# First mixer of a four-layer model: the head norm woven into the head loop, one root for six heads, the output product opened beside the last two heads

## What is computed

```python
def hgrn2_mixer(x, w_in, lb, head_gain, w_out):
    q, f_pre, i, g = jnp.split(x @ w_in, 4, axis=-1)
    ...                       # eight heads of width 128, chunks of 64 tokens, give o
    o = o * lax.rsqrt(jnp.mean(o * o, axis=-1, keepdims=True) + EPS)
    o = o * head_gain.astype(jnp.float32).reshape(A_HEADS, A_DV)
    o = o.reshape(Bsz, T, D_MODEL).astype(x.dtype) * jax.nn.silu(g)
    return o @ w_out
```

## Time and profile before

| | us |
|---|---|
| median of three runs | 1563.09 (1561.83 to 1564.55) |
| the profiled execution's own time | 1562.21 |
| its span in the trace | 1560.4 |
| TensorE busy | 1451.6 (93%) |
| VectorE busy | 1054.4 (68%) |
| ScalarE busy | 774.2 (50%) |

### The profile page before, as it was taken

One profiled execution on the slowest core, in us unless ns is written; L12 is line 12 of the kernel. 1 busy time (PEld: TensorE's weight loads), 2 busy tenths in 40 slices (PEclk: granted clock), 3 DMA queues, 4 the chain that ended last, 5 costly groups with the idle time before them and its releaser, 6 DMA issues. The chain is left out here.

```text
span 1560.4 us, 29022 instructions
## 1 busy us (share of the span) xinstructions
PE 1451.6 (93%) x11297; PEld 1392.3 (89%) x11297; DVE 1054.4 (68%) x1752; ACT 774.2 (50%) x1251; POOL 288.3 (18%) x390
## 2 busy tenths in 40 slices
PE   7998889999779997999988899989999988999997
PEld 7997889999678877999977799989999986899997
DVE  7764778886775536888777755367787666587643
ACT  6646545454454544555436555664433555544341
POOL 1001011210064420112001144002432100132110
PEclk9999999999898998999989999999999999999998
DMA  8533435569342213555962211136765733375451
GB/s 323 182 108 136 162 140 218 204 234 334 125 162 82 72 58 115 218 217 203 356 233 84 105 57 66 69 121 233 276 247 207 249 106 136 108 289 210 143 177 45
DMA packets 41860, 265.73 MB, mean 170 GB/s; under 512 B 4640, under 2 KB 5920, under 8 KB 16416
## 3 DMA queue, kind: packets, MB, share of 16 engines
q1 hardware_dynamic: 41760, 264.38, 46.8%
HBM read 263.31 MB, written 1.05 MB: 169 GB/s over the span
## 5 line engine op out<-in xcount | busy, mean ns | idle before, releaser
L224 DVE TENSOR_TENSOR w_lo<-raw,w_hi 128x2048 fp32r<-128x2048 f32 (+2 forms) x206 | 424.1, 2063 | 183.5 <-ACT w_hi L220 180.2
L220 ACT ACTIVATE w_hi<-raw 128x2048 fp32r<-128x2048 f32 (+2 forms) x223 | 384.1, 1727 | 82.0 <-PE bank L1081 43.0
L412 PE MATMUL bank<-x_hi_up,w_hi 128*128 128x272 f32 (+1 forms) x704 | 203.4, 289 | 8.3 <-DVE x_lo_up L717 8.1
L414 PE MATMUL bank<-x_hi_up,w_lo 128*128 128x272 f32 (+1 forms) x704 | 201.7, 287 | 0.0
L413 PE MATMUL bank<-x_lo_up,w_hi 128*128 128x272 f32 (+1 forms) x704 | 201.2, 286 | 0.0
L412 PE MATMUL bank<-z_hi,w_hi 128*128 128x258 f32 x704 | 200.3, 285 | 0.0
L413 PE MATMUL bank<-z_lo,w_hi 128*128 128x258 f32 x704 | 198.7, 282 | 0.0
L414 PE MATMUL bank<-z_hi,w_lo 128*128 128x258 f32 x704 | 198.0, 281 | 0.0
L412 PEld LDWEIGHTS bank<-x_hi_up,w_hi 128*128 128x128 f32 x704 | 133.3, 189 | 10.4 <-issue 8.8
L413 PEld LDWEIGHTS bank<-x_lo_up,w_hi 128*128 128x128 f32 x704 | 133.7, 190 | 0.0
L413 PEld LDWEIGHTS bank<-z_lo,w_hi 128*128 128x128 f32 x704 | 133.3, 189 | 0.1
(11 more groups left out here) (476 smaller groups left out, 3889.2 us busy)
## 6 DMA issues: line engine op xcount, KB each, us to landing
raw<-w_up SPq DMA_DIRECT2D x44, 1024.0 KB, 4.8
raw<-w_gu SPq DMA_DIRECT2D x44, 1024.0 KB, 4.8
work<-w_ada SPq DMA_DIRECT2D x27, 1024.0 KB, 5.0
raw<-w_down SPq DMA_DIRECT2D x32, 704.0 KB, 5.0
raw<-w_dn SPq DMA_DIRECT2D x32, 704.0 KB, 4.1
mod_w_down<-w_ada SPq DMA_DIRECT2D x16, 1024.0 KB, 6.1
raw<-w_a_in SPq DMA_DIRECT2D x15, 1024.0 KB, 5.0
raw<-w_gdn_qkv SPq DMA_DIRECT2D x12, 1024.0 KB, 4.9
```

The lines of the kernel that those rows point to most:

```text
L220: act.activation(w_hi[:, s, 0:blocks * P], raw[:, s, 0:blocks * P], ACT.Copy).then_inc(hi_split.sem, 1)
L224: dve.tensor_tensor(w_lo[:, s, 0:blocks * P], raw[:, s, 0:blocks * P], w_hi[:, s, 0:blocks * P].bitcast(F32), ALU.subtract).then_inc(lo_sp ...
L412: pe.matmul(o, w_hi[:, s, b], x_hi[:, xk, cols[0]:cols[1]], start=begin, stop=False)
L414: last = pe.matmul(o, w_lo[:, s, b], x_hi[:, xk, cols[0]:cols[1]], start=False, stop=end)
```

## The change

`HeadNormEntry` goes. Its work moves into `Hgrn`, and `Hgrn` and the product a_out run in one block.

- ScalarE, which copied each head's output to `v`, also squares it from bank 7 into `work`.
- A new event ("sum", m) adds up squares over the partitions. Each head's matmul has eight columns of weights (`head_pick`, a window with ones in one column), so that head j's sums fall into row j of bank 2. Group 0 is heads 0 to 5, group 1 heads 6 and 7. ScalarE takes one square root over the eight rows, VectorE one reciprocal of it.
- A new event ("spread", m) copies row j of the reciprocals to all partitions with a matmul of eight rows, alternately into banks 3 and 6. Matmul j waits until VectorE has used the bank two heads before. VectorE multiplies by gain and root from the bank, ScalarE makes the high part, VectorE the low part.
- A new event ("open", i) runs the matmuls of product item 16+i for the blocks of heads 0 to 5, 36 in all.
- The end of the order was head(10), g6, g7, head(11). Now it is head(10), sum 0, g6, spread 0, g7, head(11), open 0, sum 1, open 1, spread 1. The product's steps 16 and 17 then run only the 12 matmuls of the last two heads; steps 18 and 19 are whole.
- GpSimd multiplies output and gate as heads and gates come, beside the other engines.
- The modulation's first two transfers are issued when item 15 is done, which is at the end of g7. The tables of ScalarE change: a logarithm, an exponential and a square root behind the heads go; a square root at sum 0, silu at g6 and a square root at sum 1 come.

```diff
--- before.py
+++ after.py
@@ -758,68 +758,6 @@
...
-        class HeadNormEntry:
...
@@ -997,7 +935,16 @@
                 k_tok = sbuf(scope, "k_tok_a", [P, 2, n_chunks, P])
                 attn = sbuf(scope, "attn_a", [P, 2, 3, P])
                 state = sbuf(scope, "state_a", [P, 2, n_chunks, P])
+                head_pick = sbuf(scope, "head_pick", [P, 2 * HEADS - 1])
                 reset = con("reset_hgrn")
+                groups = [range(0, 6), range(6, HEADS)]
+                roots = [(e[0:HEADS, 0, :], e[0:HEADS, 1, :]), (b[0:HEADS, 0, :], b[0:HEADS, 1, :])]
+                mix_hi, mix_lo = mix[:, 0:KD, :], mix[:, KD:2 * KD, :]
+                pick_set, head_summed, head_std, head_rooted = (sig("tok_made"), sig("o_summed"), sig("head_logged"),
+                                                                sig("head_rstd"))
+                head_spread, head_gated, head_normed = sig("spread"), sig("head_gated"), sig("head_normed")
+                mix_high, mix_split = sig("tile_high"), sig("mixed_split")
+                self.split, self.mix_hi, self.mix_lo = mix_split, mix_hi, mix_lo
                 lb_max, lb_exp, lb_done = sig("lb_max"), sig("lb_exp"), sig("lb_done")
                 half_done, copied_out = sig("half_tile_done"), sig("tile_copied_out")
                 f_made, k_made, logged, summed = sig("f_made"), sig("k_made"), sig("f_logged"), sig("b_summed")
...
@@ -1023,8 +970,11 @@
                     if i < len(items):
                         x, m = items[i]
                         order += [tile(x, 2 * m), tile(x, 2 * m + 1)]
+                        if i == len(items) - 1:
+                            order[-2:] = [("sum", "", 0), tile(x, 2 * m), ("spread", "", 0), tile(x, 2 * m + 1)]
                     if i == HEADS:
                         order.append(("gates", "", 0))
+                order += [("open", "", 0), ("sum", "", 1), ("open", "", 1), ("spread", "", 1)]
                 turn = {event: i for i, event in enumerate(e_ for e_ in order if e_[0] == "tile")}
                 in_turn = list(turn)
                 ring_of = lambda event: starts[f"a_{event[1]}{event[2] // 2}"][0]
@@ -1135,6 +1085,27 @@
                                                  v_tok[:, y, (c + 1) // 2, :], start=True, stop=True)
                             last.then_inc(ds_done.sem, 1)
 
+                    def sum_heads(m):
+                        if m:
+                            pe.wait_ge(head_std.sem, head_std.at(m))
+                        else:
+                            pe.wait_ge(pick_set.sem, pick_set.at(2))
+                        for j in groups[m]:
+                            pe.wait_ge(o_out.sem, o_out.at(j + 1))
+                            last = pe.matmul(bank[2][0:HEADS, 0:T1], head_pick[:, HEADS - 1 - j:2 * HEADS - 1 - j], work[:, j, :],
+                                             start=j == groups[m][0], stop=j == groups[m][-1])
+                        last.then_inc(head_summed.sem, 1)
+
+                    def spread_heads(m):
+                        if m == 0:
+                            pe.wait_ge(stated.sem, stated.at(n_chunks * HEADS))
+                        pe.wait_ge(head_rooted.sem, head_rooted.at(m + 1))
+                        for j in groups[m]:
+                            if j >= 2:
+                                pe.wait_ge(head_normed.sem, head_normed.at(j - 1))
+                            pe.matmul(bank[(3, 6)[j % 2]][:, 0:T1], con("ident", j, 1, 0, HEADS).broadcast_to([HEADS, P]),
+                                      roots[m][1], start=True, stop=True).then_inc(head_spread.sem, 1)
+
                     pe.wait_ge(ones_set.sem, ones_set.at(1))
                     for event in order:
                         if event[0] == "tile":
@@ -1143,6 +1114,14 @@
                                 add_up()
                         elif event[0] == "head":
                             head(event[2])
+                        elif event[0] == "sum":
+                            sum_heads(event[2])
+                        elif event[0] == "spread":
+                            spread_heads(event[2])
+                        elif event[0] == "open":
+                            for last_two in in_turn[-2:]:
+                                tile_taken(pe, last_two)
+                            self.next_product.opening(pe, event[2])
 
                 def vector(dve):
                     def scan(j):
@@ -1209,6 +1188,17 @@
                                           ALU.add).then_inc(f_made.sem, 1)
                         dve.wait_ge(f_made.sem, f_made.at(n + 1))
                         dve.tensor_scalar(k[:, n, :], f[:, n, :], -1.0, 1.0, ALU.mult, ALU.add).then_inc(k_made.sem, 1)
+
+                    def norm_head(j):
+                        dve.wait_ge(head_spread.sem, head_spread.at(j + 1))
+                        dve.wait_ge(head_gated.sem, head_gated.at(j + 1))
+                        dve.scalar_tensor_tensor(g[:, j, :], g[:, j, :], par("head_norm", j), bank[(3, 6)[j % 2]][:, 0:T1],
+                                                 ALU.mult, ALU.mult).then_inc(head_normed.sem, 1)
+
+                    def low_head(j):
+                        dve.wait_ge(mix_high.sem, mix_high.at(j + 1))
+                        dve.tensor_tensor(mix_lo[:, j, :], g[:, j, :], mix_hi[:, j, :].bitcast(F32),
+                                          ALU.subtract).then_inc(mix_split.sem, 1)
 
                     dve.memset(eps_col[:, :], EPS).then_inc(eps_set.sem, 1)
                     dve.wait_ge(params_in.sem, 16)
@@ -1262,6 +1252,15 @@
                             scan(0)
                         elif kind == "head":
                             head(n)
+                        elif kind == "sum":
+                            dve.wait_ge(head_std.sem, head_std.at(n + 1))
+                            dve.reciprocal(roots[n][1], roots[n][0]).then_inc(head_rooted.sem, 1)
+                        elif kind == "spread":
+                            for j in groups[n]:
+                                norm_head(j)
+                                if j > groups[n][0]:
+                                    low_head(j - 1)
+                            low_head(groups[n][-1])
                     dve.wait_ge(c_ready.sem, 1)
 
                 def scalar(act):
@@ -1280,7 +1279,8 @@
                             act.activation(f[:, i - 1, :], f[:, i - 1, :], ACT.Exp).then_inc(diff_exped.sem, 1)
                         if i >= 4:
                             act.wait_ge(o_done.sem, o_done.at(i - 3))
-                            act.activation(v[:, i - 4, :], bank[7][:, 0:T1], ACT.Copy).then_inc(o_out.sem, 1)
+                            act.activation(v[:, i - 4, :], bank[7][:, 0:T1], ACT.Copy)
+                            act.activation(work[:, i - 4, :], bank[7][:, 0:T1], ACT.Square).then_inc(o_out.sem, 1)
                         if 2 <= i < HEADS + 2:
                             j, y = i - 2, i % 2
                             act.wait_ge(turned.sem, turned.at(j + 1))
@@ -1344,6 +1344,14 @@
                             act.activation(c_row[:, :], c_row[:, :], ACT.Silu).then_inc(c_ready.sem, 1)
                         elif kind == "head":
                             head(n)
+                        elif kind == "sum":
+                            act.wait_ge(head_summed.sem, head_summed.at(n + 1))
+                            act.activation(roots[n][0], bank[2][0:HEADS, 0:T1], ACT.Sqrt, scale=1.0 / P,
+                                           bias=eps_col[0:HEADS, 0:1]).then_inc(head_std.sem, 1)
+                        elif kind == "spread":
+                            for j in groups[n]:
+                                act.wait_ge(head_normed.sem, head_normed.at(j + 1))
+                                act.activation(mix_hi[:, j, :], g[:, j, :], ACT.Copy).then_inc(mix_high.sem, 1)
                     act.wait_ge(copied_out.sem, copied_out.at(len(turn)))
                     act.sem_inc(item_out.sem, len(A_ITEMS))
 
@@ -1358,9 +1366,18 @@
                     pool.memset(k_tok[:, :, :, :], 0.0)
                     pool.memset(v_tok[:, :, 0, :], 0.0)
                     pool.memset(attn[:, :, 0, :], 0.0).then_inc(cleared.sem, 1)
+                    pool.memset(head_pick[:, :], 0.0).then_inc(pick_set.sem, 1)
+                    pool.wait_ge(pick_set.sem, pick_set.at(1))
+                    pool.memset(head_pick[:, HEADS - 1:HEADS], 1.0).then_inc(pick_set.sem, 1)
+                    for j in range(HEADS):
+                        pool.wait_ge(o_out.sem, o_out.at(j + 1))
+                        pool.wait_ge(silued.sem, silued.at(max(1, j - 2)))
+                        pool.tensor_tensor(g[:, j, :], v[:, j, :], g[:, j, :], ALU.mult).then_inc(head_gated.sem, 1)
 
                 def passed():
...
         with ExitStack() as outer:
-            qfig = sbuf(outer, "qfig", [P, 4 * KD, T1])
-            q, f, v, g = (qfig[:, i * KD:(i + 1) * KD, :] for i in range(4))
```

(49 more changed lines are left out.)

9 lines of the change are left out of this document (4 added, 5 removed).

## The result

| | before | changed |
|---|---|---|
| median, first comparison | 1563.09 (1561.83 to 1565.23, 5 executions) | 1572.07 (1568.84 to 1573.35, 5) |
| median, compared again beside experiments | 1564.22 (1561.22 to 1569.31, 23) | 1568.47 (1562.34 to 1570.96, 12) |
| the profiled execution's own time | 1562.21 | 1572.08 |
| its span | 1560.4 | 1570.2 |
| its mean granted clock | 0.972 | 0.966 |

A forecast was written before the change was run, and what follows sets the result against it. TensorE, busy 93%, was taken as the bound, standing still before the product; filling that moves the root from 186.09 to 184.7, VectorE ending last. The 1.4 us gain gives a median of 1561.7 us, range 1558.8 to 1564.5.

The forecast's parts named there:

- The clock stays up: TensorE from g6 through the product: no standstill reaches 1.5 us, so the granted clock stays at 1.00, 136 to 182 us.
- The allowance behind the root: Layer behind the stretch: TensorE's clock falls and returns at other moments, allowed 1 us either way.
- The spread's pace: Spread 0 between g6 and g7: 0.76 us per head, ending some 4.0 us after g6.
- The serial rival: Each head's spread, norm, high and low parts run serially, 1.85 us per head; kernel 5.1 us slower, 1568.2; chance 0.08.
- the 147.5: Sign at tile g7 on TensorE: a start after 147.5 us would show the assumed spread pace wrong.
- The table loads: ScalarE's loads run ahead of waits, hidden; the rival puts them behind, losing the 1.4 us gain: 1563.4; chance 0.12.
- The sums: Head sums on TensorE: 0.49 us each, six before g6; root 0.49 and reciprocal 1.85 us, eight rows costing what 128 do.
- VectorE sets the end: Product's end: VectorE starts at 165.4, works 19.0 us without a gap; root at 184.7, gain 1.4 us.
- the first rival: TensorE sets the end: root at 183.2, gain 2.9 us, 3.5 with favourable clock, 1560.2 to 1559.6; chance 0.15.
- GpSimd's multiplies: Output-gate multiplies beside VectorE: only head 6's falls into a chain, 0.2 us allowed, bounds 0 to 0.75.
- the filled standstill: TensorE's wait before the product, filled by the change: its root 2.9 us earlier, half given back to VectorE.

The follow-up runs named there:

- e6: Kernel before the change plus 14 unused back-to-back matmuls on 8 rows between g6 and g7: 1579.25 us, ratio 1.0094.
- e7: Kernel before the change plus 14 unused back-to-back matmuls on 128 rows between g6 and g7: 1572.89 us, ratio 1.0059.
- e1: Changed kernel with the spread matmuls on 128 rows, zeros added, instead of 8: 1565.04 us, ratio to the kernel before 0.9993.
- e5: Changed kernel unedited, measured again with more executions beside the kernel before: 1568.47 us, ratio 1.0021.
- e3: Changed kernel with 128-row spreads and the product not opened beside the last heads: 1568.0 us, ratio to the kernel before 1.0016.
- e2: Kernel before the change plus one unused 400-column VectorE reciprocal ahead of the one behind the root: 1569.17 us, ratio 1.002.
- e4: Changed kernel with 128-row spreads and weight item 19 split earlier, beside open 0: 1563.01 us, ratio to the kernel before 0.9983.
- e8: As e4, with one of VectorE's modulation columns also moved beside open 1: 1563.35 us, ratio to the kernel before 0.9986.

## Why the prediction was wrong

- **The step that failed** is "The clock stays up, since no standstill here reaches 1.5 us: the one of 1.2 us ahead of the head sums left it at 1.00 over 145 to 150 us." Its premise held: TensorE stood 0.18 us in spread 0 and 1.2 in front of the product. The conclusion didn't: the clock fell to 0.50 at 146.8 us with TensorE busy, since matmuls on 8 rows did not hold it up even back to back (e6 against e7), and with 128 rows it stayed at 1.00 (e1). The rows quoted for it had only matmuls of 128 rows and could not show that. I costed the 8-row spread by its columns alone; in the earlier trace rows there was none to compare with, and that is where a doubt about the clock belonged, as a rival. Cost: 1.8 to 3.4 us at the root, and 3.5 us in the means (e5's 1568.1 against e1's 1564.6; the two ran on different chips, on which the kernel before had means of 1564.9 and 1564.8).
- **The allowance behind the root**, "From the spread of the three runs I allow 1 us for it either way", was too small as well. Three executions spanned 2.7 us, thirty-five 10.3. The profiled execution of the changed kernel has the low stretch at 570 us, 3.1 us, and a wider one at 1324 to 1331; those of before, e3, e6 and e7 don't have the first, those of e1, e2, e4, e5 and e8 do, whether their root was early or late. What decides it is open.
- **The spread's pace** held. In the changed kernel the norms repeat after 0.76 us (145.40, 146.16, 146.92), and in e1 spread 0 takes 143.04 to 147.29, 4.25 against the forecast's 4.0. The serial rival is out. In the changed kernel g7 starts at 147.86, past the 147.5 that was to show a wrong pace, but there it is the clock and 0.67 us of start; in e1 it starts at 146.93.
- **The table loads** run ahead of the waits, as the earlier trace rows had it, so that rival is out too. ScalarE's timeline of the changed kernel, with the load of the square root 2.28 us ahead of its instruction:

```profile
137.89 1.28 ACT L1349 ACT_TABLE_LOAD   x1
140.17 0.48 ACT L1349 ACTIVATE decay<-bank,eps_col 8x272 f32<-8x272 f32 x1 [1.00 <-PE bank L1095]
140.67 1.28 ACT L1335 ACT_TABLE_LOAD   x1
```

- **The sums**: 2.92 us for six, forecast 6 x 0.49. The reciprocal on eight rows took 1.84 us, against 1.85 on 128, the root 0.48, against 0.49, as assumed.
- **VectorE sets the end**: in e1 its first split comes at 166.03 (forecast 165.4, and 0.5 of start), its four steps take 18.9 us (19.0), the root comes at 185.25 (184.7, and 0.5). In the changed kernel the same four take 18.8 from 169.61, without idle. With VectorE relieved, e4's root, less 0.3 of start, is at 183.3, where the first rival had it at 183.2. This part of the sum was right to 0.1 us, for a kernel whose clock stays up, which the changed one isn't.
- **GpSimd's multiplies**: 0.2 us was allowed. Head 6's took its plain 0.76 and the low part beside it 0.46. Head 5's took 2.48 us, here and in the traces of e1, e3, e4, e5 and e8, beside VectorE's split from 136.88 to 139.17. The rule of the Trainium skill weighed in the prediction (SBUF — State Buffer, section Who interferes with whom) has it so, and the trace agrees. It fell on GpSimd at a place where nobody waits:

```profile
137.31 2.48 POOL L1375 TENSOR_TENSOR vg<-vg 128x272 f32<-128x272 f32 x1 [3.62 <-ACT vg L1335]
144.42 0.76 POOL L1375 TENSOR_TENSOR vg<-vg 128x272 f32<-128x272 f32 x1 [4.63 <-ACT vg L1335]
```

- **What stays open.** e1 has the stretch as forecast, 1.3 us earlier at the root, but its time can't be told from before (interval -3.6 to +1.4 us). Whether the gain arrives at the end is not shown; the spread between executions is larger. Of the 9.8 us between the two profiled spans the runs explain the part up to the root, 2.0 us and 0.67 of start; for the 7.1 us behind it they show low stretches of the clock and no cause.

## What to carry to other kernels

When a change puts matmuls of few rows into a full TensorE stretch, don't cost them by their columns only: ask what the clock does behind them, and if the operands allow it use all 128 rows with zeros, which cost the same time per matmul and here saved 3.5 us in the means. Read who sets the end of a stretch after the edit before counting the filled standstill as gain: of 2.9 us, VectorE's queue gave back 1.5. After an edit that relieves one engine, read whether its own end moved (in e8 it didn't). And where a kernel's executions spread by more than the expected gain, compare dozens, and say of a single trace only what its own stretch shows.

## What the runs showed of the hardware

- The granted clock fell from 1.00 to 0.50 with TensorE busy without a gap, when it ran matmuls of 8 rows (e6, at about 144.5 us); the same ones on 128 rows left it at 1.00 (e7). The six matmuls of spread 0 agree: on 8 rows the clock fell inside them in both traces (146.8 and 147.0 us), on 128 rows it stayed at 1.00 in all four (e1, e3, e4, e8). Whether something between, 64 rows, would hold it was not tried.
- Until the clock fell the two kinds ran at about the same pace (10 recorded in each from 141 to 143 us), so fewer rows gained no time in the stream.
- The mean granted clock of one unchanged kernel varied between 0.965 and 0.975 over 35 executions, and its time by 10.3 us with it.
- A GpSimd multiply of 272 columns took 2.48 us instead of 0.76 while a VectorE split of 2.29 us, with both inputs in SBUF, ran beside it.
